# Down projections of two layers by Strassen's seven products, in a hybrid-layer network on one core

## The chip, the cores and the metric

The kernel runs on one core of a Trainium2 chip. The metric is the time of one execution on the device, in microseconds (us); lower is better. Engines are named as the profile names them: PE (TensorE, with PEld for its weight loads), DVE (VectorE), ACT (ScalarE), POOL (GpSimd), SP (SyncE, which issues most transfers here). SBUF is the on-chip memory of all engines, PSUM the one of eight banks that PE writes.

## The reference

512 tokens of width 1024 go through two hybrid layers (chunk attention, a convolution and retention side by side, then an MLP) and then one block of another kind. The change touches the MLP of the two layers:

```python
h = rms_norm(x, g_mlp_pre)                                  # (512, 1024)
f = jnp.square(jax.nn.relu(h @ w_up)) @ w_down              # w_up (1024, 4096), w_down (4096, 1024)
return x + rms_norm(f, g_mlp_post)
```

All is float32. The two layers are computed one after the other, each with its own weights.

## The kernel before

**Products.** PE multiplies float32r operands. To keep float32 accuracy each operand is split in a high part (a rounding copy) and a low part (operand minus high part), and each product is three matmuls: high by high, high by low, low by high. `accumulate` (line 717, matmul in line 723) issues them. A matmul has 128 x 128 stationary numbers and 512 moving columns and adds to one PSUM bank.

**Weights.** They come from memory in units of 128 x 2048 numbers (1 MB), by SP, into two buffers `raw` in turn (`load`, lines 412 to 420). ACT copies a unit to `w_hi` (`hi`, line 1412), then POOL subtracts to give `w_lo` (`lo`, line 534, or in four pieces of 512 columns, `lo_pieces`, line 526) and frees the `raw` buffer with the semaphore `split_ready`, which lets SP load the next unit. There are two `w_hi` and two `w_lo`, so ACT may write one only after PE has read it: `hi("half")` waits until PE is through the first unit of a product, `hi(7)` until bank 7 is full.

**The MLP.** The 4096 hidden features are cut in eight groups of 512. For each group g an "up" makes the hidden features (two units of `w_up`, 8 blocks of 128 inputs, 4 banks: 8 x 4 x 3 = 96 matmuls into banks 0 to 3), and a "down" multiplies them with 512 rows of `w_down` (two units of 512 output columns each; per unit 4 token tiles x 4 blocks x 3 = 48 matmuls into banks 4 to 7). `mlp_order` (line 170) sets PE's order: up(g+1) stands ahead of down(g), so that the other engines have an up's time for the hidden group. The first up (`first_group`, line 815) runs inside the norm before it.

**Beside PE.** DVE rectifies and scales a full bank into `hid` (line 2339), ACT squares it (line 1714) and makes its high part (line 1715), DVE its low part (`low`, line 2169). In the first group of a layer ACT also clears `f` with two copies of 2048 columns (line 1718). After each down DVE adds banks 4 to 7 to `f` in SBUF (line 2353, 128 x 512 each, eight per group). After the last down ACT sums squares (line 1444), DVE makes the scales (lines 2037 to 2041), and PE turns and scales `f` (line 795) into the next norm.

**Order in POOL's queue.** In layer 1 it is one `lo` per unit, in a loop. In layer 2 POOL also computes tables that the later block needs: `output_tables` (line 573) and `turns` (line 604), 37 tensor_tensor operations of 128 x 512 with both inputs in SBUF. They are generators; after each of 18 yields one `lo` follows.

Every engine runs its own list of instructions in order. A wait in it holds all that stands behind it.

```python
def mlp_order(eng, c, up, down, n, per):
    up(0, 0)
    def body(j):
        up(2 * j + 1, 1)
        down(2 * j, 0)
        up(2 * j + 2, 0)
        down(2 * j + 1, 1)
```

Of the kernel before, what the change touches and what calls it, by code (L numbers as in the profile page):

```python
# [13 lines left out]

# [12 lines left out]
P = 128  # L27
# [39 lines left out]
for _name, _w in (("g0", KD), ("g2", KD), ("qg", 1), ("kg", 1), ("subln", 1), ("a_re", NS), ("a_im", NS),  # L67
# [35 lines left out]
PER_PASS = dict(  # L103
    act_step=8, free0=2, free1=2, free2=2, free3=2, free4=4, free5=4, free6=4, free7=4, full0=2,
    full1=2, full2=2, full3=2, full4=4, full5=4, full6=4, full7=4, h_hi=8, h_lo=8, half_done=2,
    split_ready=8, w_loaded0=64, w_loaded1=64)
# [82 lines left out]

def build(nc, a, out):  # L190
# [36 lines left out]
    "f_clear",  # L227
    "table_made",
# [54 lines left out]
def memory(nc):  # L283
# [53 lines left out]
    m.diag = ar("diag", [P, NT, P], 14)  # L337
# [18 lines left out]
    m.h_lo = [ar(f"h_lo{i}", [P, 4, T], 8 + 16 * i, F32R) for i in range(2)]  # L356
    m.both_first = ar("both_first", [P, T], 56)
# [45 lines left out]
def loads(sp, a, m, s, out):  # L403
# [8 lines left out]
    def load(*parts):  # L412

        slot = unit[0] % 2
        unit[0] += 1
        apart(sp, s["split_ready"], c.up("split_ready"), s["slot_seen"])
        for to, of in parts:
            sp.dma_start(to(m.raw[slot]), of).then_inc(s[f"w_loaded{slot}"], 16)
        if beside:
            beside.pop(0)()  # L420
# [13 lines left out]
    def layer(l):  # L434
# [27 lines left out]
        def up(g, _):  # L462
            column_group(a["w_up"], l, g * GROUP)

        def down(g, _):
            for half in range(2):
                load((into(KU, GROUP), rows(a["w_down"], l, g * GROUP, KU, half * GROUP, GROUP)))

        mlp_order(sp, c, up, down, N_UP, PER_PASS)
# [43 lines left out]
def low_parts(pool, m, s):  # L513
# [14 lines left out]

    def lo(n=UNIT):
# [26 lines left out]
    def pre_norm():  # L556

        lo()
        add_squares(1, 2, 3, 4, 5, 6)
        lo()  # L560
# [69 lines left out]
    def layer(l):  # L630
# [12 lines left out]
        pre_norm()  # L643
        if l < DEPTH - 1:
            passes(pool, c, U_MLP // 2 - 2, PER_PAIR, pair)
        else:
            for _ in range(4):
                lo()
            for _ in output_tables():
                lo()  # L650
            lo()
            for _ in turns(0):
                lo()
            for _ in range(U_MLP - 4 - 4 - 15 - 3):
                lo()
        lo()
        lo_pieces()
        pre_norm()

# [34 lines left out]
def products(pe, m, s):  # L694
# [240 lines left out]

    def layer(l):
# [36 lines left out]
        def up(g, i):  # L973
            if isinstance(g, int) and g == 0:
                first_group()
            else:
                feature_major(4)

        def down(g, i):
            pe.wait_ge(s["h_lo"], c.up("h_lo", 4))  # L980
            for half in range(2):
                wh, wl = weights(next_unit(), KU, GROUP)
                for t in range(NT):
                    tt = slice(t * P, (t + 1) * P)
                    accumulate(4 + t, bank[4 + t][:], [(m.h_hi[i][:, k, tt], m.h_lo[i][:, k, tt], wh[:, k, :], wl[:, k, :])
                                                       for k in range(KU)], True, True, False)

        mlp_order(pe, c, up, down, N_UP, PER_PASS)
# [206 lines left out]
NEW, NEW_POST = (5, 6, 7), (4, 5, 6, 7)  # L1195
BUSY = (1, 4, 22, 4)
# [169 lines left out]
def functions(act, a, m, s):  # L1366
# [72 lines left out]
    def post_square(k, x):  # L1439

        if k >= 4:
            act.wait_ge(s["post_squared"], c.at("post_squared") - 3)
        c.up("post_squared")
        act.activation(m.squares[k % 4][:], x, ACT.Square, accum_out=m.half_sums[:, k:k + 1]).then_inc(s["post_squared"], 1)
# [5 lines left out]

    def post_half(squared, copied=None):

        for t in range(NT):
            squared(NT + t)
            if t == 2:
                post_root(0, 2)
            if t == 3:
                post_root(2, 4)
            if copied:
                copied(t)  # L1460
# [34 lines left out]
    def pre_norm(gain):  # L1495

        for k in range(KD):
# [6 lines left out]
            if k == 5:  # L1504
                hi("half")
# [149 lines left out]
    def layer(l):  # L1655
# [45 lines left out]
        post_half(squared, copied)  # L1701
        act.wait_ge(s["layer_loaded"], c.up("layer_loaded", 16))
        pre_norm(gain("g_mlp"))

        def up(g, i):
            use(0, 1, 2, 3)
            if isinstance(g, int) and g == 0:
                act.wait_ge(s["full3"], c.at("full3"))
                hi()
            else:  # L1710
                hi("half")
            for b in range(4):
                freed(b)
                link(act.activation(m.hid[:, b, :], m.hid[:, b, :], ACT.Square))
                act.activation(m.h_hi[i][:, b, :], m.hid[:, b, :], ACT.Copy).then_inc(s["h_hi"], 1)
            if isinstance(g, int) and g == 0:
                for half in range(2):
# [3 lines left out]
        def down(g, i):  # L1721
            hi(7)
            use(4, 5, 6, 7)
            if isinstance(g, int) and g == N_UP - 1:
                for k in range(NT):
                    summed(k)
# [1058 lines left out]
```

## Time and profile before

| | us |
|---|---|
| runs of the kernel: median of 3 (lowest, highest) | 2116.07 (2110.57, 2118.12) |
| the profiled execution, its own time | 2113.84 |
| its span in the trace | 2112.0 |
| PE busy | 2066.0 |
| DVE, ACT, POOL busy | 1033.8, 881.0, 891.0 |
| mean granted TensorE clock, share of full | 0.995 |

The profile is of one execution. "Busy" of PE counts overlapping matmuls once and is not a measure of how full the array is. A row of a group of instructions gives line, engine, operation, output<-input by the program's names, shapes and count, then busy time and mean length, then the idle time of that engine before them and what ended it. A row of the timeline begins with start and length in us; brackets hold the idle time before it.

### The profile page before, as it was taken

Reading aid. Unit: us, or ns where it says so; the run is one execution under the profiler, and the core shown is the slowest. Engines: PE = TensorE matmul, PEld = TensorE weight load, DVE = VectorE, ACT = ScalarE, POOL = GpSimd, SP = SyncE. Lnnn points to the kernel's source line nnn. Section 1 sums busy time; section 2 is a strip of 40 time slices with the busy share of each in tenths; the row PEclk is TensorE's granted clock in tenths of the full one; section 3 lists DMA queues with packets and bytes.
Section 4 is the critical chain, followed back from the end, with each engine's and each line's share of the span. In section 5 each row is a group of like instructions: output and inputs, shape, how many; then the busy total and the mean of one; then the engine's idle time right before and its main releaser. Section 6 shows DMA issues by size and latency. Waiting matters only on the chain.

```text
span 2112.0 us, 27508 instructions
## 1 busy us (share of the span) xinstructions
PE 2066.0 (98%) x10240; PEld 1659.4 (79%) x10240; DVE 1033.8 (49%) x1713; ACT 881.0 (42%) x1257; POOL 891.0 (42%) x282
## 2 busy tenths in 40 slices
PE   8999999999999999999999998999999999999999
PEld 7875888888888775888888886777776787888887
DVE  5866242222236764232222248886589634464555
ACT  5345562223344445542322352265476434333332
POOL 5533244444435323445665446224222344444442
PEclk9999999999999999999999998999999999999999
DMA  5432123322224321223323224232211222332232
GB/s 180 156 110 80 60 81 99 101 90 91 97 75 156 127 90 54 67 100 100 99 89 104 88 83 148 86 90 90 80 61 60 100 100 80 100 99 87 92 99 80
DMA packets 120050, 202.29 MB, mean 96 GB/s; under 512 B 6545, under 2 KB 51857, under 8 KB 119697
## 3 DMA queue, kind: packets, MB, share of 16 engines
q1 hardware_dynamic: 112992, 189.12, 27.3%
q10 hardware_dynamic: 6960, 11.88, 2.0%
q8 instruction: 60, 0.98, 0.2%
q14 instruction: 38, 0.30, 0.0%
HBM read 189.44 MB, written 8.12 MB: 94 GB/s over the span
## 4 chain that ended last, share of the span: by engine, by line
PE 75%; issue 15%; DVE 5%; POOL 3%; ACT 1%; DMA 0%; ACTq 0%; DVEq 0%; POOLq 0%; SPq 0%
PE bank L723 63%; PE bank L837 5%; POOL w_lo L534 3%; PE bank L848 1%; PE bank L795 1%; PE bank L906 1%; PE bank L866 1%; PE bank L894 1%; PE bank L1040 0%; DVE w L2449 0%; DVE pr L2107 0%; PE bank L777 0%; PE bank L932 0%; POOL sums L550 0%; DVE w L2443 0%
## 5 line engine op out<-in xcount | busy, mean ns | idle before, releaser
L534 POOL TENSOR_TENSOR w_lo<-raw,w_hi 128x2048 fp32r<-128x2048 f32 (+1 forms) x167 | 742.2, 4444 | 1151.8 <-ACT w_hi L1412 1151.8
L1412 ACT ACTIVATE w_hi<-raw 128x2048 fp32r<-128x2048 f32 (+1 forms) x170 | 314.3, 1849 | 582.5 <-PE bank L723 528.1
L723 PE MATMUL bank<-act_hi,w_hi 128*128 128x512 f32 x1296 | 516.5, 399 | 3.7 <-DVE hid L2658 2.5
L723 PE MATMUL bank<-act_hi,w_lo 128*128 128x512 f32 x1296 | 506.5, 391 | 0.0
L723 PE MATMUL bank<-act_lo,w_hi 128*128 128x512 f32 x1296 | 506.4, 391 | 0.0
L723 PEld LDWEIGHTS bank<-act_hi,w_hi 128*128 128x128 f32 x1296 | 244.3, 189 | 67.0 <-issue 12.2
L723 PEld LDWEIGHTS bank<-act_hi,w_lo 128*128 128x128 f32 x1296 | 244.2, 188 | 52.4
L723 PEld LDWEIGHTS bank<-act_lo,w_hi 128*128 128x128 f32 x1296 | 244.6, 189 | 49.3 <-issue 1.0
L723 PE MATMUL bank<-w_hi,h_hi 128*128 128x512 f32 x512 | 199.2, 389 | 0.0
L723 PE MATMUL bank<-w_lo,h_hi 128*128 128x512 f32 x512 | 199.2, 389 | 0.0
L723 PE MATMUL bank<-w_hi,h_lo 128*128 128x512 f32 x512 | 199.2, 389 | 0.0
L2353 DVE TENSOR_TENSOR f<-f,bank 128x512 f32<-128x512 f32 x128 | 87.9, 687 | 225.1 <-PE bank L723 225.1
L2339 DVE SCALAR_TENSOR_TENSOR hid<-bank,rrow 128x512 f32<-128x512 f32 x64 | 43.7, 691 | 250.2 <-PE bank L723 245.1
L723 PE MATMUL bank<-w_hi,act_hi 128*128 128x512 f32 (+1 forms) x320 | 120.6, 377 | 0.0
L723 PE MATMUL bank<-w_hi,act_lo 128*128 128x512 f32 (+1 forms) x320 | 117.6, 368 | 0.0
L723 PE MATMUL bank<-w_lo,act_hi 128*128 128x512 f32 (+1 forms) x320 | 117.6, 368 | 0.0
L723 PEld LDWEIGHTS bank<-w_hi,h_lo 128*128 128x128 f32 x512 | 96.1, 188 | 20.0
L723 PEld LDWEIGHTS bank<-w_hi,h_hi 128*128 128x128 f32 x512 | 96.1, 188 | 20.0
L723 PEld LDWEIGHTS bank<-w_lo,h_hi 128*128 128x128 f32 x512 | 96.1, 188 | 19.9
L2653 DVE TENSOR_TENSOR bank<-bank,rrow 128x512 f32<-128x512 f32 x44 | 30.7, 699 | 142.5 <-PE bank L723 139.9
L837 PE MATMUL bank<-act_hi,w_hi 128*128 128x512 f32 x192 | 78.5, 409 | 4.2 <-DVE act_lo L2029 3.4
L2082 DVE SCALAR_TENSOR_TENSOR bank<-ypad,lcol,bank 128x512 f32<-128x512 f32 x116 | 76.6, 753 | 0.0
(393 smaller groups left out, 3078.3 us busy)
## 6 DMA issues: line engine op xcount, KB each, us to landing
raw<-in_w_up SPq DMA_DIRECT2D x32, 1024.0 KB, 5.5
raw<-in_w_down SPq DMA_DIRECT2D x32, 1024.0 KB, 5.0
raw<-in_w_in SPq DMA_DIRECT2D x26, 1024.0 KB, 5.2
raw<-in_w_up SPq DMA_DIRECT2D x44, 512.0 KB, 4.5
raw<-in_w_in SPq DMA_DIRECT2D x28, 768.0 KB, 4.6
raw<-in_w_out SPq DMA_DIRECT2D x12, 1024.0 KB, 5.0
raw<-in_w_down SPq DMA_DIRECT2D x22, 512.0 KB, 4.2
raw<-in_w_attn_proj SPq DMA_DIRECT2D x4, 1024.0 KB, 5.0
```

The source lines that it names most:

```text
L534: pool.tensor_tensor(m.w_lo[slot][:, 0:n], m.raw[slot][:, 0:n], m.w_hi[slot][:, 0:n].bitcast(F32), ALU.subtract).then_inc(s["split_ready"], 1)
L723: mm = pe.matmul(o, ll if i == 2 else lh, rl if i == 1 else rh, start=first and n == 0, stop=last and n == len(steps) - 1)
L795: mm = pe.matmul(bank[b][:, t * P:(t + 1) * P], m.f[:, 4 * (k // 4) + t, k % 4 * P:(k % 4 + 1) * P], m.diag[:, t, :], start=True, stop=True)
L837: mm = pe.matmul(bank[b][:], (wl if i == 2 else wh)[:, k % KU, cols], (m.act_lo if i == 1 else m.act_hi)[:, k, :], start=(k == 0 and i == ...
L848: pe.matmul(bank[b][:] if o is None else o, lhsT, rhs, start=True, stop=True).then_inc(s[f"full{b}"], 1)
L866: mm = pe.matmul(bank[b][head(h), j * P:T], m.rv[:, j, h * HD:(h + 1) * HD], m.pr[:, 2 * (i % 2) + comp, 0:T - j * P], start=(j == 0), sto ...
L894: mm = pe.transpose(bank[6][:, kc * P:(kc + 1) * P], m.pr[:, 2 * (step % 2) + comp, kc * P:(kc + 1) * P], m.ident)
L1412: act.activation(m.w_hi[slot][:, 0:n], m.raw[slot][:, 0:n], ACT.Copy).then_inc(s["w_hi"], 1)
L2082: ins = dve.scalar_tensor_tensor(to, y, w, sums, ALU.mult, ALU.add)
L2339: dve.scalar_tensor_tensor(m.hid[:, b, :], bank[b][:], 0.0, m.rrow[:], ALU.max, ALU.mult).then_inc(s[f"free{b}"], 1)
L2353: dve.tensor_tensor(sums, sums, bank[4 + b][:], ALU.add).then_inc(s[f"free{4 + b}"], 1)
L2653: dve.tensor_tensor(bank[b][:], bank[b][:], m.rrow[:], ALU.mult).then_inc(s["up_scaled"], 1)
```

## The change

In seven of the eight groups of a layer the down projection (512 tokens x 512 features by 512 features x 1024 outputs) is done with Strassen's algorithm in the form with shared sums. Both operands are cut in quarters: h in 256 tokens x 256 features, w_down in 256 rows x 512 columns. Seven products of quarters, or of sums of quarters, take the place of eight. A product is two token tiles x 2 blocks x 3 = 12 matmuls in two banks, 84 for a group. Products 3, 5 and 7 add onto the banks of products 1, 3 and 5 while those still hold their sum, and product 6 onto those of product 4, so the sums of products cost no instruction. DVE adds each bank after each product to `f`: 14 additions for a group. The last group is done as an ordinary product (96 matmuls), now in an order by token tile, with eight banks.

Sums of quarters: four of h (128 x 512 numbers each) and four of w_down (128 x 1024 each), all by DVE, all with both inputs in SBUF. High parts of the seven factors of either operand are made by ACT, low parts of h's factors by DVE, those of w_down's by POOL (128 x 1024 each). The factors of w_down use the halves of the two `w_hi`/`w_lo` buffers as four slots: 0, 1, 2, 3, 0, 1, 2. Slots 2 and 3 are the buffer that the up in front of the down reads to its end.

`mlp_steps` takes the place of `mlp_order`: a loop of six steps and one more, each an up and then a down. Units of `w_down` now hold 256 rows of all 1024 columns. The first unit of an up is split by POOL in four pieces. Layer 2's tables stand in POOL's queue from the second step on, three places for each step: behind factor 0, behind factor 1, and behind the second unit of the next up. ACT's sums of squares in the norms write one scrap tile and wait for each other.

The diff, cut to its core:

```diff
+FACTORS = [((4, 5), 0), ((6, 7), 1), ((4, 5), 2), ((6, 7), 3), ((4, 5), 0), ((6, 7), 1), ((4, 5), 2)]
+SUM_OF = (0, 0, 4, 6, 6, 4, 2)
+def mlp_steps(eng, c, step, last):
+    passes(eng, c, N_UP - 2, PER_STEP, step)
+    last()
 # SP
+        def down(g):
+            for r in range(2):
+                load((into(2, D), rows(a["w_down"], l, g * GROUP + r * 2 * P, 2, 0, D)), loaded="d_loaded")
+        def step(g):
+            column_group(a["w_up"], l, (g + 1) * GROUP)
+            down(g)
 # POOL
+    def factor_lo(n, of):
+        pool.wait_ge(s["w_hi"], c.up("w_hi"))
+        pool.tensor_tensor(half_slot(m.w_lo, n), of, half_slot(m.w_hi, n).bitcast(F32), ALU.subtract).then_inc(s["q_lo"], 1)
+    def mlp_step(beside=(), last=False):
+        factor_lo(0, quarter(m.raw[0], 0))
+        next(beside, None)
+        factor_lo(1, quarter(m.raw[1], 0))
+        next(beside, None)
+        pool.wait_ge(s["t_made"], c.up("t_made", 4))
+        raw_free()
+        factor_lo(2, m.w_sum[0][:])
+        factor_lo(3, m.w_sum[1][:])
+        factor_lo(0, m.w_sum[2][:])
+        factor_lo(1, quarter(m.raw[1], 1))
+        raw_free()
+        factor_lo(2, m.w_sum[3][:])
...
+            lo_quarters(4)
+        lo()
+        next(beside, None)
...
-            for _ in output_tables():
-                lo()
-            lo()
-            for _ in turns(0):
-                lo()
+            tables = itertools.chain(output_tables(), turns(0))
+            for g in range(N_UP - 1):
+                mlp_step(tables if g else (), g == N_UP - 2)
 # PE
+    def down():
+        ready = c.at("h_lo")
+        for p, (banks, n) in enumerate(FACTORS):
+            wh, wl = (half_slot(w, n) for w in (m.w_hi, m.w_lo))
+            if p < 3:
+                pe.wait_ge(s["h_lo"], ready + (p + 1 if p < 2 else 7))
+            pe.wait_ge(s["q_lo"], c.up("q_lo"))
+            for j, b in enumerate(banks):
+                fill(b)
+                tt = slice(j * P, (j + 1) * P)
+                for k in range(2):
+                    for i in range(3):
+                        mm = pe.matmul(bank[b][:], (m.q_lo if i == 2 else m.q_hi)[:, p, k, tt], (wl if i == 1 else wh)[:, k, :],
+                                       start=(p in (0, 1, 3) and k == 0 and i == 0), stop=(k == 1 and i == 2), skip_group_check=True)
+                mm.then_inc(s[f"full{b}"], 1)
 # ACT
+        def step(last=False):
+            act.wait_ge(s["hid_ready"], c.up("hid_ready", 4))
+            h_part(0, x(0, 0))
+            h_part(1, x(1, 0))
+            for p, of in ((3, m.h_sum[:]), (4, x(0, 1)), (2, x(0, 0)), (5, x(1, 0))):
+                act.wait_ge(s["h_sum"], c.up("h_sum"))
+                h_part(p, of)
+            h_part(6, x(1, 1))
+            act.wait_ge(s["half_done"], c.up("half_done"))
+            act.wait_ge(s["d_loaded0"], c.up("d_loaded0", 16))
+            factor_hi(0, quarter(m.raw[0], 0))
+            act.wait_ge(s["d_loaded1"], c.up("d_loaded1", 16))
+            factor_hi(1, quarter(m.raw[1], 0))
+            use(0, 1, 2, 3)
+            for b in range(3):
+                squares(b)
+            act.wait_ge(s["full3"], c.at("full3"))
+            act.wait_ge(s["t_made"], c.up("t_made", 4))
+            factor_hi(2, m.w_sum[0][:])
+            squares(3)
+            factor_hi(3, m.w_sum[1][:])
...
+            done(5, 3)
+            half_hi(0, 0)
+            done(7, 3)
+            half_hi(0, 1)
+            done(5, 4)
+            act.activation(m.w_hi[1][:], m.raw[1][:], ACT.Copy).then_inc(s["w_hi"], 1)
 # DVE
+        def h_factors():
+            link(dve.tensor_tensor(m.h_sum[:], x(0, 1), x(1, 1), ALU.add), "h_sum")
+            link(dve.tensor_tensor(x(0, 1), x(0, 0), x(0, 1), ALU.subtract), "h_sum")
+            h_low(0, x(0, 0))
+            h_low(1, x(1, 0))
+            link(dve.tensor_tensor(x(0, 0), m.h_sum[:], x(0, 0), ALU.subtract), "h_sum")
+            link(dve.tensor_tensor(x(1, 0), x(1, 0), x(0, 0), ALU.subtract), "h_sum")
+            for p, of in ((3, m.h_sum[:]), (4, x(0, 1)), (2, x(0, 0)), (5, x(1, 0)), (6, x(1, 1))):
+                h_low(p, of)
+        def w_factors():
+            wait("d_loaded0", 16)
+            wait("d_loaded1", 16)
+            link(dve.tensor_tensor(m.w_sum[1][:], b12, b11, ALU.subtract), "t_made")
+            link(dve.tensor_tensor(m.w_sum[2][:], b22, b12, ALU.subtract), "t_made")
+            link(dve.tensor_tensor(m.w_sum[0][:], b22, m.w_sum[1][:], ALU.subtract), "t_made")
+            link(dve.tensor_tensor(m.w_sum[3][:], b21, m.w_sum[0][:], ALU.subtract), "t_made")
+        def step(last=False):
+            h_factors()
+            w_factors()
+            for b in range(4):
+                rectify(b)
+            for p in range(7):
+                for j in range(2):
+                    add_factor(p, j)
+                if last and p >= 3:
+                    low(m.l_lo[p - 3][:], m.act2[:, p - 3, :], m.l_hi[p - 3][:], "h_hi", "h_lo")
```

`quarter` and `half_slot` give a quarter of a `raw` buffer and a half of a `w_hi`/`w_lo` buffer, `raw_free` frees a `raw` buffer for SP, `done(b, n)` waits until bank b has been filled n times in this step, `link` waits for the instruction just issued.

## Rows read from the trace of the kernel before

**Rows 1.** The page's busy times (share of the span) and its chain by line

```profile
PE 2066.0 (98%) x10240; PEld 1659.4 (79%) x10240; DVE 1033.8 (49%) x1713; ACT 881.0 (42%) x1257; POOL 891.0 (42%) x282
...
PE bank L723 63%; PE bank L837 5%; POOL w_lo L534 3%; PE bank L848 1%; PE bank L795 1%; PE bank L906 1%; PE bank L866 1%; PE bank L894 1%; PE bank L1040 0%; DVE w L2449 0%; DVE pr L2107 0%; PE bank L777 0%; PE bank L932 0%; POOL sums L550 0%; DVE w L2443 0%
```

**Rows 2.** Timeline of PE and DVE: start, length, instruction

```profile
312.58 0.39 PE L723 MATMUL bank<-w_hi,h_hi 128*128 128x512 f32 x1
...
320.06 0.39 PE L723 MATMUL bank<-w_hi,h_hi 128*128 128x512 f32 x1
...
348.21 0.69 DVE L2339 SCALAR_TENSOR_TENSOR hid<-bank,rrow 128x512 f32<-128x512 f32 x1 [12.91 <-PE bank L723]
...
356.91 2.49 DVE L2169 TENSOR_TENSOR h_lo<-hid,h_hi 128x512 fp32r<-128x512 f32 x4
...
391.66 0.69 DVE L2339 SCALAR_TENSOR_TENSOR hid<-bank,rrow 128x512 f32<-128x512 f32 x1 [12.84 <-PE bank L723]
```

**Rows 3.** Groups by shape, ACT; timelines of ACT and of PE's first up

```profile
L1412 ACT ACTIVATE w_hi<-raw 128x2048 fp32r<-128x2048 f32 x144 | 275.6, 1914 | 534.1 <-PE bank L723 499.8 <-issue 18.5 <-DMA raw<-in_w_in 9.9
...
296.73 0.63 ACT L1715 ACTIVATE h_hi<-hid 128x512 fp32r<-128x512 f32 x1
297.27 3.70 ACT L1718 ACTIVATE f<-kcol 128x2048 f32<-128x2048 f32 x2
...
290.69 0.50 PE L723 MATMUL bank<-act_hi,w_hi 128*128 128x512 f32 x1
```

**Rows 4.** Tile w_lo on POOL: count, ns min/median/max

```profile
L534 POOL TENSOR_TENSOR w_lo<-raw,w_hi x167: 3473/4606/5078, 19.5 to 2088.3; 128x2048 fp32r<-128x2048 f32 x141, 128x1536 fp32r<-128x1536 f32 x26
...
L526 POOL TENSOR_TENSOR w_lo<-raw,w_hi x12: 1281/1290/1609, 10.9 to 1223.8; 128x512 fp32r<-128x512 f32 x12
```

**Rows 5.** Two tiles on DVE: count, ns min/median/max

```profile
L2353 DVE TENSOR_TENSOR f<-f,bank x128: 679/687/690, 315.8 to 1227.6; 128x512 f32<-128x512 f32 x128
...
L2169 DVE TENSOR_TENSOR h_lo<-hid,h_hi x86: 678/684/3967, 293.9 to 2096.2; 128x512 fp32r<-128x512 f32 x86
```

**Rows 6.** Groups by shape, DVE: one line at two widths

```profile
L2107 DVE TENSOR_TENSOR pr<-bank,decay 128x512 f32<-128x512 f32 x12 | 7.7, 686 | 27.3 <-PE bank L848 27.3
...
L2107 DVE TENSOR_TENSOR pr<-bank,decay 128x384 f32<-128x384 f32 x12 | 6.1, 550 | 0.0
```

**Rows 7.** Timeline of DVE and POOL where both have work

```profile
1425.83 5.12 DVE L2494 TENSOR_TENSOR k<-k,rope 128x512 f32<-128x512 f32 x1
...
1425.66 4.73 POOL L534 TENSOR_TENSOR w_lo<-raw,w_hi 128x2048 fp32r<-128x2048 f32 x1 [6.75 <-ACT w_hi L1412]
...
1302.66 1.43 DVE L2492 TENSOR_TENSOR partner<-partner,rope 128x512 f32<-128x512 f32 x1
1304.01 1.54 DVE L2494 TENSOR_TENSOR q<-q,rope 128x512 f32<-128x512 f32 x1
...
1303.50 1.50 POOL L617 TENSOR_TENSOR both<-turn_table,turn_table 128x512 f32<-128x512 f32 x1
```

**Rows 8.** Groups by shape, POOL: busy us, mean ns; a table with a broadcast input

```profile
L595 POOL TENSOR_TENSOR c_part<-ctab,par 128x512 f32<-128x512 f32 x4 | 4.2, 1050 | 0.3
```

**Rows 9.** Timeline of PE, and one us of the windows (third from last: PEclk)

```profile
17.92 0.47 PE L837 MATMUL bank<-act_hi,w_hi 128*128 128x512 f32 x1 [2.38 <-DVE act_lo L2029]
...
19.15 0.63 PE L837 MATMUL bank<-act_hi,w_lo 128*128 128x512 f32 x1
...
22.56 0.39 PE L837 MATMUL bank<-act_lo,w_hi 128*128 128x512 f32 x1
...
620.30 2.05 PE L795 MATMUL bank<-diag,f 128*128 128x128 f32 x16 [0.99 <-DVE diag L2041]
...
21.00:22.00 1.00, 1.00 (x4) 0.81 (x3) 0.55 (x1) 1.00 (x3) 1.00 (x1) 0.50 0.00 0
```

**Rows 10.** The page's transfers: count, size, us to landing

```profile
raw<-in_w_up SPq DMA_DIRECT2D x32, 1024.0 KB, 5.5
raw<-in_w_down SPq DMA_DIRECT2D x32, 1024.0 KB, 5.0
```

More of the change, by code:

```diff
@@ L460, in layer @@
             column_group(a["w_out"], l, g * GROUP)
[L462 to L469, printed above, removed]
+        def down(g):
[4 more added lines that the diff above has]
+            down(g)
+        column_group(a["w_up"], l, 0)
+        mlp_steps(sp, c, step, lambda: step(N_UP - 2))
+        down(N_UP - 1)
     for l in range(DEPTH):
@@ new lines, in last_down, with tile @@
+    def last_down():
+        def tile(i, u, k):
+            t, half = divmod(i, 2)
+            cols, tt = slice(half * SW, (half + 1) * SW), slice(t * P, (t + 1) * P)
+            for n in range(3):
+                mm = pe.matmul(bank[(4 + i) % 8][:], (m.l_lo if n == 2 else m.l_hi)[2 * u + k][:, tt],
+                               (m.w_lo if n == 1 else m.w_hi)[u][:, k * D:(k + 1) * D][:, cols],
+                               start=(u == 0 and k == 0 and n == 0), stop=(u == 1 and k == 1 and n == 2))
+            return mm
+        unit[0] += 1
+        for k in range(2):
+            if k == 0:
+                pe.wait_ge(s["lo_piece"], c.up("lo_piece"))
+            else:
+                pe.wait_ge(s["split_ready"], c.up("split_ready"))
+            pe.wait_ge(s["h_lo"], c.up("h_lo"))
+            for i in (4, 5, 6, 7, 2, 3, 0, 1):
+                if k == 0:
+                    fill((4 + i) % 8)
+                mm = tile(i, 0, k)
+        mm.then_inc(s["half_done"], 1)
+        next_unit()
+        pe.wait_ge(s["h_lo"], c.up("h_lo", 2))
+        for i in range(8):
+            for k in range(2):
+                mm = tile(i, 1, k)
+            mm.then_inc(s[f"full{(4 + i) % 8}"], 1)
@@ L971, in layer @@
         post_norm()
[L973 to L988, printed above, removed]
+        first_group()
+        mlp_steps(pe, c, lambda g: (up(), down()), lambda: (up(), down()))
+        last_down()
         post_norm()
@@ L1740, in functions @@
+        mlp_steps(act, c, lambda g: step(), lambda: step(last=True))
+        c.up("hid_ready", 4)
+        c.up("h_hi", 4)
+        use(0, 1, 2, 3, 4, 5, 6, 7)
+        hi("half")
+        for i in range(8):
+            act.wait_ge(s["f_done"], c.up("f_done"))
+            post_square(i, m.f[:, 4 * (i % 2) + i // 2, :], 4 * (i % 2) + i // 2)
+            if i == 4:
+                post_root(0, 2)
+        post_root(2, 4)
+        pre_norm(gain("g_next"), lambda: hi("half"))
     act.wait_ge(s["eps_loaded"], 16)
@@ L2346, in down @@
-        def down(g, i):
-            for half in range(2):
-                for b in range(4):
-                    freed(4 + b)
-                    full(4 + b)
-                    sums = m.f[:, 4 * half + b, :]
-                    dve.tensor_tensor(sums, sums, bank[4 + b][:], ALU.add).then_inc(s[f"free{4 + b}"], 1)
-                    if isinstance(g, int) and g == N_UP - 1:
-                        freed(4 + b)
-                        dve.sem_inc(s["f_done"], 1)
-                        if half == 1 and b == 2:
-                            post_diag(0, 2)
@@ new lines, in layer @@
+        for b in range(4):
+            rectify(b)
+        wait("f_clear", 2)
+        mlp_steps(dve, c, lambda g: step(), lambda: step(last=True))
+        c.up("hid_ready", 4)
+        c.up("d_loaded0", 16)
+        c.up("d_loaded1", 16)
+        for i in range(8):
+            b = (4 + i) % 8
+            full(b)
+            sums = m.f[:, 4 * (i % 2) + i // 2, :]
+            dve.tensor_tensor(sums, sums, bank[b][:], ALU.add).then_inc(s[f"free{b}"], 1)
+            freed(b)
+            dve.sem_inc(s["f_done"], 1)
+            if i == 4:
+                post_diag(0, 2, 4)
```

232 lines of the change are left out of this document (153 added, 79 removed).

## The prediction

> **What bounds the kernel now.** First the page's busy times and its chain: PE is busy in 98% of the span, the others in 42 to 49%; in the chain that ended last, the matmuls of line 723 alone have 63% [rows 1]. So the time is PE's, and the half-idle engines look like free room: in an average over the span they are. The 0.39 us of a matmul [rows 2] are not its price: matmuls overlap, and in order of time they start every (320.06 - 312.58) / 33 = 0.2267 us [rows 2]. One group (96 up and 96 down matmuls) then takes 192 x 0.2267 = 43.5 us; the same rectify stands at 348.21 and at 391.66 [rows 2], 43.45 apart with a loop end between, so bank changes, waits and loop ends cost PE nothing.
>
> **What the change removes.** Seven products of 12 matmuls take the place of 96, in 7 groups of both layers: 14 x 12 = 168 matmuls, 168 x 0.2267 = 38.1 us. The matmul's shape stays (128 x 128 by 512). A step (up, then down) becomes 180 x 0.2267 = 40.8 us: up 21.8, each product 2.72, down 19.0. The last group stays ordinary.
>
> **What it adds, per step.** ACT takes 1.91 us for 2048 columns and 0.63 for 512 [rows 3], by a line between them 1.06 for 1024. It now has nine pieces of 1024 (seven factors of w_down, two halves of w_up), one of 2048, seven parts of h and four squares: 9.5 + 1.9 + 4.4 + 2.5 = 18.3 us. POOL takes 4.6 and 1.29 (medians [rows 4]), so 2.4 for 1024: seven factors 16.8, four quarters 5.2, one whole unit 4.6, in all 26.6 us, where four units took 18.5. DVE: 14 adds and 4 rectifies at 0.69 [rows 2, 5], 7 low parts of h at 0.61 (four took 2.49 [rows 2]), 4 sums of h at 0.72 (0.69 and a hand-over, since each is waited for), and 4 sums of w of 1024 columns, not in the trace: 0.686 for 512 and 0.550 for 384 [rows 6] give 0.136 per 128 columns, 1.23 in all; bounds 0.69 (no longer than 512) and 1.37 (twice it). That is 18 x 0.69 + 11 x 0.66 + 4 x 1.23 = 24.6 us. By these totals every engine has room under PE's 40.8.
>
> **What stands against hiding.** A DVE instruction with both inputs in SBUF doesn't run beside a POOL tensor_tensor. One of 0.69 took 5.12: it began 0.17 after a POOL piece of 4.73 and ended 0.56 after it [rows 7]. Where both have work queued they alternate: DVE's 0.69 takes 1.43 and 1.54, POOL's 1.05 takes 1.50, and in turn one ends 0.91 and the other 0.55 after the one before [rows 7]. A low part of h has once taken 3.97; the 128 adds that read PSUM lie between 0.679 and 0.690, so they are never held [rows 5]. Today four low parts per group lie clear of POOL. The change puts 15 such instructions (4 sums and 7 low parts of h, 4 sums of w) into each up, where three of POOL's pieces must come too. By the Trainium skill, page SBUF — State Buffer, section Who interferes with whom, a DVE instruction with two SBUF inputs and a GpSimd one that reads SBUF exclude each other for the whole instruction, and with one SBUF input don't contend; by that rule sharing is impossible in all these pairs, and the trace agrees.
>
> **Chain of a plain step**, laid out from those durations in each engine's own order, in us from the start of up. PE's last bank of the down before is seen after 0.46, when ACT makes w_hi of slot 1, to 2.4; POOL, held 0.2 by a sum of h, 2.6 to 7.2. DVE's seven low parts and two linked sums wait for it: 7 x 0.61 + 2 x 0.72 = 5.7, to 12.9. POOL's factor 0 (ACT has it at 12.4) 12.9 to 15.1; first sum of w to 16.3; factor 1 to 18.5; three sums of w, 3.7, to 22.2. Only now can DVE rectify the new h, which its order puts behind the sums: three banks take 1.9, to 24.0 (PE had filled them at 13.6 to 19). ACT squares the third, to 24.7, and turns to factor 2, which its order puts behind those squares: to 25.7. POOL makes the low part, to 28.2. PE wants it after up and two products, 21.8 + 5.4 = 27.2. Stall 1.0, and 0.2 for loading the weights: **1.2**. If the sums of w all came ahead of factor 1, they would end 2.3 earlier and nothing would be late: the low bound is 0. With POOL a tenth slower (2.6 for 1024) it is 3.3, the high one. Later factors have slack: each is wanted 2.72 after the one before, POOL makes one in 2.4.
>
> The first step of a layer starts behind the clearing of f: two of 1.9 from 297.27, with four h_hi copies of 0.63 before them gone [rows 3], end 8 us after the start of up (290.69 [rows 3]). Behind them come the 11 instructions of DVE on h (7.2), factors 0 and 1 (2.3 each), the sums of w (4.9), three rectifies (1.9), a square (0.6), ACT's and POOL's part of factor 2 (1.1 + 2.5): 30.8, with hand-overs 31.2, which is 4.0 late; **4.2**.
>
> **Layer 2's tables.** POOL also computes 37 table operations there of 1.05 (a broadcast input [rows 8]) or 1.29 us (as a piece of 512 [rows 4]), before beside whole units, now six in each of steps 2 to 7: two behind the unit of 4.6, two behind factor 0, two behind factor 1. Five of them come in turn ahead of the last sum of w. Five times 1.05 is 5.2; I take 4.5, since ACT is ready a little later too. That stall is 1.0 + 4.5 + 0.2 = **5.7**. Step 2 has no pair behind the unit and waits 1.8; the last 5.5. Bounds: 1.0 per step if the two engines never leave the shared access idle (POOL 26.6 + 7.0, DVE 12.5, less 33 overheads of 0.69 - 0.56 = 0.13 [rows 7], is 41.8 against 40.8), and 6.5 if all six count.
>
> Stalls: layer 1 4.2 + 6 x 1.2 = 11.4; layer 2 4.2 + 1.8 + 4 x 5.7 + 5.5 = 34.3; 45.7 in all.
>
> **The clock.** After 2.38 us of idle PE the starts went from 0.23 to 0.43 apart from 19.15 to 22.56, the granted clock at 0.50, that is 1.2 GHz, and 2.4 GHz again from there by the lengths of 0.39 [rows 9]. Eight matmuls lose 0.2 each, 1.6 in all. A wait of 0.99 stands in the trace with 16 matmuls of 128 columns in 2.05 behind it, 0.13 each, too fast for half the clock [rows 9]; so I let plain stalls lose nothing. Seven stalls are over 3 us: 7 x 1.6 = 11.2; bounds 0 and 8 x 1.6.
>
> **At nothing.** Weights: a load lands 5.0 to 5.5 us after issue [rows 10]; w_down's second unit, asked for at 7.4, is there at 12.7, when ACT comes to it; the tightest is the next group's second, free behind factor 5 at 35.4, there 41.2, wanted at 42.5. If late, 1 us per step. The loads' rows are longer, their bytes the same. Squares one after another in the norms: banks fill every 2.7 us, a square with its read takes 0.8. The last down keeps 96 matmuls; its tail is add, square, root, diag as before (the 0.99 [rows 9]). Bounds -1 and +3 in all.
>
> **Sum.** -38.1 + 45.7 + 11.2 = +18.8. The profiled execution took 2113.84, span 2112.0; so 2132.6. The runs' median is 2.2 higher, inside their spread of 7.5; I say 2133.
>
> **Rivals.**
> Everything hides (the totals decide): if alternation lets DVE's sums through early, no stall stays, 2113.8 - 38.1 = 2076, up to 2090 with the two first steps. For it: the totals. Against: DVE held for whole pieces [rows 7]. Chance 0.15.
> Half: plain steps hide, since 1.0 is small beside 27, and the tables find gaps at 2.5 per step with no clock loss: -38.1 + 8.4 + 15 = -15, 2099. Chance 0.12.
> Level: stalls as worked out, but no clock loss or shorter table stalls: 2113.8 + 3 = 2117 (2104 to 2124). Chance 0.18.
> Forecast, 2124 to 2146: chance 0.42.
> Worse: port overheads add up, every plain step loses 3.3 as with slower POOL (+14 per layer), and next loads come late: 2133 + 28 = 2161, from 2146 on. Chance 0.13.
> That the change does not save its matmuls I give nothing: 84 against 96 is written in the table of products.
>
> About 0.5%, 10.6 us, is what a measurement of this kernel tells from no change. Faster: 0.15 + 0.12 = 0.27; same 0.18; slower 0.55. The range leaves out the first rival and the worst part of the last: 2094 to 2152. The forecast's own is 2124 to 2146.
>
> **What would show it.** PE has 10072 matmuls, busy share some 95%. Right: PE idle ahead of the third product's first matmul, put down to POOL's w_lo; about 1 us in layer 1, 5 to 6 in layer 2, and 4 in each first step; matmuls 0.43 apart behind the long ones; DVE's sums of w with means near 2 us instead of 1.23; layer 2's steps near 48 us, layer 1's near 42. Wrong: steps of 40.8 in both layers (port not binding); DVE's two-SBUF instructions at 0.69 beside POOL; stalls at another product or ahead of up (loads or the next unit late); no 0.50 clock in layer 2.

## The result and the profile after

The changed kernel took **2128.8 us** (median of 5 runs, 2125.79 to 2135.43), the kernel before 2115.45 beside it (5 runs): a ratio of **1.0074**, 95% interval 1.0049 to 1.0098. The change is slower, by 0.7%, though it takes 168 matmuls out. The profiled execution took 2128.65, its span is 2126.9, 14.9 more than before's 2112.0.

The page of the changed kernel, busy times and chain by engine, against [rows 1]:

```profile
PE 2043.2 (96%) x10072; PEld 1634.9 (77%) x10072; DVE 1348.1 (63%) x1951; ACT 942.4 (44%) x1385; POOL 1041.4 (49%) x396
...
PE 58%; issue 21%; DVE 14%; POOL 5%; ACT 2%; ACTq 0%; DVEq 0%; DMA 0%; POOLq 0%; SPq 0%
```

and the chain by engine of the kernel before:

```profile
PE 75%; issue 15%; DVE 5%; POOL 3%; ACT 1%; DMA 0%; ACTq 0%; DVEq 0%; POOLq 0%; SPq 0%
```

The matmuls are gone, and yet the span has grown: DVE and POOL, 8% of the chain before, now have 19%. The waits of PE say where (engine, line, waited for: us in all, times, longest), of the whole span and then of each layer's MLP:

```profile
PE bank L1042 <- POOL w_lo L574: 33.2, 12, 5.1
PE bank L1042 <- issue: 4.9, 3, 2.6
...
PE bank L1042 <- POOL w_lo L574: 6.9, 6, 3.3
PE bank L1042 <- issue: 0.6, 1, 0.6
...
PE bank L1042 <- POOL w_lo L574: 26.3, 6, 5.1
PE bank L1042 <- issue: 4.3, 2, 2.6
```

So 7.5 us of idle PE in layer 1 and 30.6 in layer 2, all ahead of the third product's first matmul but one stall: in layer 2's last step PE waits 2.59 ahead of the second product and then 1.74 ahead of the third. One place of each layer, in the timeline of PE:

```profile
404.26 0.50 PE L1042 MATMUL bank<-w_hi,q_hi 128*128 128x512 f32 x1 [0.72 <-POOL w_lo L574]
404.60 0.39 PE L1042 MATMUL bank<-w_lo,q_hi 128*128 128x512 f32 x1
...
1063.35 0.79 PE L1042 MATMUL bank<-w_hi,q_hi 128*128 128x512 f32 x1 [5.14 <-POOL w_lo L574]
1063.94 0.63 PE L1042 MATMUL bank<-w_lo,q_hi 128*128 128x512 f32 x1
1064.37 0.63 PE L1042 MATMUL bank<-w_hi,q_lo 128*128 128x512 f32 x1
```

Behind the stall of 0.72 the next matmul starts 0.34 after the first and the one after that 0.23 later, as at full speed. Behind 5.14 they start 0.43 apart (the first even 0.59), and the granted clock of the window (third number from the end) is the lower level, 1.2 GHz:

```profile
1064.00:1066.00 2.00, 2.00 (x6) 0.50 0.00 0
```

53 matmuls of the two MLPs are slow in this way, 7 behind layer 1's first stall and 46 in layer 2: 53 x 0.2 = 10.6 us.

The span by stretches, from the same landmarks in both traces (times in us from the span's start, the kernel before's in brackets): the first up of layer 1 starts 2.5 earlier than before (288.19 against 290.69 [rows 3]); the norm's second token matmuls close layer 1's MLP at 609.90 (620.30 [rows 9]), 7.9 gained in that MLP; the same place of layer 2 is at 1244.92 (1230.37), 25.0 lost since; 0.4 more to the end. -2.5 - 7.9 + 25.0 + 0.4 = 15.0, the 14.9 of the spans with rounding. **Layer 1 gains what layer 2 more than loses**, although both layers run one code on PE, ACT and DVE; only POOL's differs, by the tables. A step takes 41.8 us in layer 1 and 48.0 in layer 2, for 180 x 0.2267 = 40.8 of matmuls.

How the stall of a layer 2 step comes about, in the timelines of DVE, POOL and ACT:

```profile
1095.50 2.07 DVE L2544 TENSOR_TENSOR w_sum<-raw 128x1024 f32<-128x1024 f32 x1
1097.61 2.20 DVE L2545 TENSOR_TENSOR w_sum<-raw,raw 128x1024 f32<-128x1024 f32 x1
1099.84 3.30 DVE L2546 TENSOR_TENSOR w_sum<-raw,w_sum 128x1024 f32<-128x1024 f32 x1
1103.18 1.96 DVE L2547 TENSOR_TENSOR w_sum<-raw,w_sum 128x1024 f32<-128x1024 f32 x1
1105.26 2.48 DVE L2522 SCALAR_TENSOR_TENSOR act<-bank,rrow 128x512 f32<-128x512 f32 x4
...
1094.99 1.50 POOL L675 TENSOR_TENSOR c_part<-ctab,par 128x512 f32<-128x512 f32 x1
1096.57 2.15 POOL L676 TENSOR_TENSOR ctab<-ctab,c_part 128x512 f32<-128x512 f32 x1
1098.80 3.26 POOL L574 TENSOR_TENSOR w_lo<-raw,w_hi 128x1024 fp32r<-128x1024 f32 x1
1102.02 2.03 POOL L669 TENSOR_TENSOR ctab<-ctab,par 128x512 f32<-128x512 f32 x1
1104.13 1.91 POOL L670 TENSOR_TENSOR c_part<-ctab,par 128x512 f32<-128x512 f32 x1
1108.83 2.36 POOL L574 TENSOR_TENSOR w_lo<-w_sum,w_hi 128x1024 fp32r<-128x1024 f32 x1 [2.78 <-ACT w_hi L1846]
...
1105.98 1.82 ACT L1843 ACTIVATE act<-act 128x512 f32<-128x512 f32 x3 [12.74 <-DVE act L2522]
1107.71 1.04 ACT L1846 ACTIVATE w_hi<-w_sum 128x1024 fp32r<-128x1024 f32 x1
```

The two engines take turns through all of it: by starts and lengths each instruction ends 0.9 to 1.2 us behind the other engine's (2.3 for POOL's low part of 1024 columns), and DVE's four sums of w take 9.5 us. Behind the last sum there follow, in series, the rectifies, three squares of ACT, its copy to 1108.8 and POOL's low part to 1111.2; PE starts at 1111.32. In layer 1 there is nothing on POOL beside the last two sums, and by groups of its six steps (count | busy us, mean ns) they show their true length:

```profile
L2544 DVE TENSOR_TENSOR w_sum<-raw 128x1024 f32<-128x1024 f32 x6 | 20.5, 3420 | 0.0
L2545 DVE TENSOR_TENSOR w_sum<-raw,raw 128x1024 f32<-128x1024 f32 x6 | 19.8, 3301 | 0.2
L2546 DVE TENSOR_TENSOR w_sum<-raw,w_sum 128x1024 f32<-128x1024 f32 x6 | 7.3, 1225 | 0.2
L2547 DVE TENSOR_TENSOR w_sum<-raw,w_sum 128x1024 f32<-128x1024 f32 x6 | 7.3, 1225 | 0.2
```

Layer 2's last step is another case. Between POOL's factor 0 and factor 1 four table operations stand there, not two: `output_tables` ends without a yield, so the same place also takes the first two operations of `turns`. Factor 1 (1198.39) is done at 1201.62, and the second product's first matmul starts at 1201.71:

```profile
1190.58 1.50 POOL L675 TENSOR_TENSOR c_part<-ctab,par 128x512 f32<-128x512 f32 x1
1192.15 2.15 POOL L676 TENSOR_TENSOR ctab_end<-ctab_end,c_part 128x512 f32<-128x512 f32 x1
1194.49 1.83 POOL L691 TENSOR_TENSOR sin_n<-turn_table,turn_table 128x512 f32<-128x512 f32 x1 [0.18 <-POOL ctab_end L676]
1196.27 2.04 POOL L692 TENSOR_TENSOR both_first<-turn_table,turn_table 128x512 f32<-128x512 f32 x1
1198.39 3.23 POOL L574 TENSOR_TENSOR w_lo<-raw,w_hi 128x1024 fp32r<-128x1024 f32 x1
...
1201.71 0.47 PE L1042 MATMUL bank<-w_hi,q_hi 128*128 128x512 f32 x1 [2.59 <-issue]
```

### The profile page after: what moved, and what is told of

Same layout as the page of the kernel before. It is cut to its first block, busy times and chain, and to the rows that moved or that the text cites. A ratio compares the mean times of both kernels' runs of the same rounds, so it can differ in the third digit from the quotient of the medians.

```text
span 2126.9 us, 28005 instructions
## 1 busy us (share of the span) xinstructions
PE 2043.2 (96%) x10072; PEld 1634.9 (77%) x10072; DVE 1348.1 (63%) x1951; ACT 942.4 (44%) x1385; POOL 1041.4 (49%) x396
## 4 chain that ended last, share of the span: by engine, by line
PE 58%; issue 21%; DVE 14%; POOL 5%; ACT 2%; ACTq 0%; DVEq 0%; DMA 0%; POOLq 0%; SPq 0%
PE bank L795 33%; PE bank L1042 10%; PE bank L909 5%; POOL w_lo L610 3%; DVE q_lo L2354 3%; PE bank L1053 2%; DVE w_sum L2544 2%; DVE w_sum L2545 1%; PE bank L920 1%; POOL w_lo L574 1%; DVE w_sum L2546 1%; PE bank L1022 1%; DVE w_sum L2547 1%; PE bank L867 1%; PE bank L978 1%
## 5 line engine op out<-in xcount | busy, mean ns | idle before, releaser
L610 POOL TENSOR_TENSOR w_lo<-raw,w_hi 128x2048 fp32r<-128x2048 f32 (+1 forms) x123 | 541.4, 4402 | 853.9 <-ACT w_hi L1542 840.6
L795 PE MATMUL bank<-act_hi,w_hi 128*128 128x512 f32 x1072 | 428.8, 400 | 3.6 <-DVE hid L2883 2.5
L795 PE MATMUL bank<-act_lo,w_hi 128*128 128x512 f32 x1072 | 418.9, 391 | 0.0
L1542 ACT ACTIVATE w_hi<-raw 128x2048 fp32r<-128x2048 f32 (+1 forms) x112 | 203.2, 1815 | 268.0 <-PE bank L795 194.2
L795 PEld LDWEIGHTS bank<-act_lo,w_hi 128*128 128x128 f32 x1072 | 202.3, 189 | 40.9 <-issue 1.0
L1042 PE MATMUL bank<-w_hi,q_hi 128*128 128x512 f32 x392 | 159.4, 407 | 38.1 <-POOL w_lo L574 33.2
L574 POOL TENSOR_TENSOR w_lo<-w_sum,w_hi 128x1024 fp32r<-128x1024 f32 x56 | 133.1, 2397 | 78.3 <-ACT w_hi L1846 75.4
L1042 PE MATMUL bank<-w_lo,q_hi 128*128 128x512 f32 x392 | 157.5, 402 | 0.0
L1042 PE MATMUL bank<-w_hi,q_lo 128*128 128x512 f32 x392 | 157.1, 401 | 0.0
L574 POOL TENSOR_TENSOR w_lo<-raw,w_hi 128x1024 fp32r<-128x1024 f32 x42 | 115.4, 2755 | 72.2 <-ACT w_hi L1846 71.7
L2354 DVE TENSOR_TENSOR q_lo<-act,q_hi 128x512 fp32r<-128x512 f32 x84 | 122.8, 1515 | 3.1 <-ACT q_hi L1849 2.9
```

Of the source, the lines that this page charges most:

```text
L574: pool.tensor_tensor(half_slot(m.w_lo, n), of, half_slot(m.w_hi, n).bitcast(F32), ALU.subtract).then_inc(s["q_lo"], 1)
L610: pool.tensor_tensor(m.w_lo[slot][:, 0:n], m.raw[slot][:, 0:n], m.w_hi[slot][:, 0:n].bitcast(F32), ALU.subtract).then_inc(s["split_ready"], 1)
L795: mm = pe.matmul(o, ll if i == 2 else lh, rl if i == 1 else rh, start=first and n == 0, stop=last and n == len(steps) - 1)
L1042: mm = pe.matmul(bank[b][:], (m.q_lo if i == 2 else m.q_hi)[:, p, k, tt], (wl if i == 1 else wh)[:, k, :], start=(p in (0, 1, 3) and k == ...
L1542: act.activation(m.w_hi[slot][:, 0:n], m.raw[slot][:, 0:n], ACT.Copy).then_inc(s["w_hi"], 1)
L2354: dve.tensor_tensor(to, of, hi_part.bitcast(F32), ALU.subtract).then_inc(s[name], 1)
```

## The experiments

All start from the changed kernel, except the control, which starts from the kernel before. The kernel before ran beside each group: its medians were 2116.74 (first four), 2115.77 (next two) and 2113.73 (last two). Theory (A in the expectations): the third product waits for a chain in series, whose sums of w are stretched by turns with POOL because both operands lie in SBUF, and the tables add turns. Rivals (B, another in each experiment): POOL simply has too much work; the tables only fill idle time; the slow matmuls wait for something else.

**The factor ahead of the squares** (e1)

```diff
-            for b in range(3):
-                squares(b)
             act.wait_ge(s["full3"], c.at("full3"))
             act.wait_ge(s["t_made"], c.up("t_made", 4))
             factor_hi(2, m.w_sum[0][:])
-            squares(3)
+            for b in range(4):
+                squares(b)
             factor_hi(3, m.w_sum[1][:])
```

> ScalarE copies the third product's factor (the first sum of w) before it squares the rectified tiles, and no longer after three squares; nothing else is changed. Theory A (the third product waits for a chain in series: VectorE's sums of w, the rectifies, three squares, the copy, GpSimd's subtraction): 3 to 4 us leave the chain in each step, so layer 1's stalls of 0.7 us go and layer 2's of 5.1 us fall to 1.5 to 4 us; about 18 us less than the changed kernel's 2128.8, near 2111, a little under the kernel before. Theory B (GpSimd has too much work in a step whatever the order): layer 2's stalls stay within 1 us of 5.1, the time falls by under 6 us.

Measured: **2101.25** (6 runs), ratio to before 0.9926 (0.9908 to 0.9943). Four lines moved on one engine turn the change from a loss into a gain. PE's waits for w_lo over the whole span:

```profile
PE bank L1042 <- POOL w_lo L574: 13.7, 7, 2.7
```

Layer 1 keeps one stall (0.85, the first step's), layer 2's plain ones fall from 5.1 to at most 2.7; the last step's 2.59 and 1.74 stay. DVE's sums are as long as they were (the step at 1076.31: 2.07, 2.19, 3.30, 1.96), POOL has the same work. So the order did it, and POOL's load as such doesn't bound. The size was off: 27.6 us less, not 18. Idle time in the two MLPs fell by 20, from 38.1 to 18.0 (layer 1's first stall too, from 3.28 to 0.85, which I had not counted), and 41 of the 53 slow matmuls went, another 8.

**No tables** (e2)

```diff
-            tables = itertools.chain(output_tables(), turns(0))
+            tables = zeros()
```

Left out: the second block's table values; `zeros` fills their tiles with zeros, three memsets at the third place of a step.

> The 37 operations by which GpSimd makes the second block's tables beside layer 2's steps are left out; 12 fills with zeros stand in their place, after each step's last subtraction. Theory A (the tables and VectorE's sums lengthen each other by taking turns, and a table operation stands ahead of the factor's subtraction): layer 2's steps become layer 1's, 41.8 to 42.5 us in place of 48.0, its MLP near 323 us in place of 354.2, and the time near 2098 (30 us less). Theory B (layer 2 waits for its own sums and copies, the tables only fill idle time): under 8 us less, 2121 or more.

Measured: **2100.37** (4 runs), ratio 0.9926 (0.9909 to 0.9943), 28.4 less than the changed kernel. Layer 2's stalls become 3.67, then 0.80 or 0.81 in each step, and a step 41.9. So the tables are the whole difference of layer 2's plain steps from layer 1's (41.8), as expected, and the last step's stall went with them (0.59 is left).

**One operand out of SBUF** (e3). Left out: the sums of w have other values.

```diff
-            link(dve.tensor_tensor(m.w_sum[1][:], b12, b11, ALU.subtract), "t_made")
+            p = m.quad[:, 0:2, :]
+            link(dve.tensor_tensor(m.w_sum[1][:], b12, p, ALU.is_gt), "t_made")
...
+            if p == 0:
+                pe.wait_ge(s["t_made"], c.up("t_made", 4))
             if p < 3:
```

`quad` names PSUM banks. The other three sums change likewise; none reads another sum any more.

> The four sums of quarters of w keep their size and their output but read the second operand from two PSUM banks, and compare in place of subtracting; the first product waits for them so that the banks hold still. The values of w's sums are not the reference's. Theory A (two operands in SBUF let VectorE and GpSimd run only in turn): the sums fall from a mean of 2.2 to 2.6 us (layer 1: 3.4, 3.3, 1.2, 1.2) to about 1.2 us each in both layers; layer 1's stalls go, layer 2's fall from 5.1 to 1 to 3 us, and the time to about 2090. Theory B (the length is that of 128x1024 elements and its queue, not the second operand's place): the sums keep 2.2 us or more beside GpSimd and the time stays within 6 us of 2128.8.

Measured: **2081.58** (4 runs), ratio 0.9843 (0.9822 to 0.9866). The four sums in layer 2's steps, by groups, with the tables and POOL's low parts beside them as before:

```profile
L2547 DVE TENSOR_TENSOR w_sum<-raw,bank 128x1024 f32<-128x1024 f32 x6 | 7.3, 1208 | 0.0
L2548 DVE TENSOR_TENSOR w_sum<-raw,bank 128x1024 f32<-128x1024 f32 x6 | 7.3, 1221 | 0.2
L2549 DVE TENSOR_TENSOR w_sum<-raw,bank 128x1024 f32<-128x1024 f32 x6 | 7.3, 1221 | 0.2
L2550 DVE TENSOR_TENSOR w_sum<-raw,bank 128x1024 f32<-128x1024 f32 x6 | 7.3, 1220 | 0.2
```

From 9.5 us to 4.9 in each step, same size, same queue, same neighbours: what stretched them was the second operand's place. (The comparison is no quicker in itself: with nothing beside it a subtraction took 1.225, see layer 1's groups.) With that alone, the squares and tables where they were, no product waits over 0.2 us for w_lo any more, and the time is 8 less than expected; what PE now waits for the sums themselves is 1.8 in all, in the two first steps. The rule of the Trainium skill that the prediction drew on (SBUF — State Buffer, Who interferes with whom) has two halves: two SBUF inputs beside POOL contend, one doesn't. The runs agree with both: 1.96 to 3.42 us beside POOL with two, 1.21 to 1.22 with one.

**Dummies ahead of the stall** (e4)

```diff
+            if p == 2 and dummies:
+                busy(16)
             pe.wait_ge(s["q_lo"], c.up("q_lo"))
```

with `dummies` set in layer 2 alone. `busy(16)` issues 16 matmuls of 128 columns on the identity (two records each in the trace, x32).

> In layer 2 only, TensorE runs 16 matmuls of 128 columns on the identity (0.275 us each) ahead of its wait for the third product's factor. Theory A (the 8 to 10 slow matmuls after each of layer 2's stalls are the half clock that follows an idle TensorE): the first matmuls after the stall keep 0.227 us, 7 x 0.2 = 1.4 us back in each of the steps that stall by 5 us, less up to 2.2 us in the one step whose stall is shorter than the dummies; 4 to 8 us less, near 2123. Theory B (the slow matmuls wait for something else, as the weights' arrival): they stay at 0.43 us, and the time is the same or 2 to 3 us longer.

Measured: **2125.26** (5 runs), ratio 1.0036 (1.0021 to 1.0050). Timeline of PE:

```profile
1103.33 3.84 PE L885 MATMUL bank<-cmat 128*128 128x128 f32 x32 [0.43 <-DVE act L2524]
1108.06 0.49 PE L1044 MATMUL bank<-w_hi,q_hi 128*128 128x512 f32 x1 [0.90 <-POOL w_lo L574]
1108.39 0.39 PE L1044 MATMUL bank<-w_lo,q_hi 128*128 128x512 f32 x1
1108.62 0.40 PE L1044 MATMUL bank<-w_hi,q_lo 128*128 128x512 f32 x1
```

The stall is as long as it was (0.43 + 3.84 + 0.90 = 5.17), but the matmuls behind it are 0.23 apart; steps take 46.3 instead of 48.0. From layer 1's norm landmark to layer 2's it takes 628.3 against 635.0. So the slow matmuls were the clock behind an idle PE. The medians show only 3.5 us of these 6.7, just under the 4 to 8 that I expected, and the intervals of the two ratios overlap, so here the trace decides and not the time: the profiled run of this kernel came to layer 1's first stall 3.5 later than the changed kernel's.

**First and moved** (e5): e1's order, and 4 pairs of tables ahead of layer 2's first step, 7 behind its MLP, one behind each later step.

```diff
         factor_lo(0, quarter(m.raw[0], 0))
-        next(beside, None)
         factor_lo(1, quarter(m.raw[1], 0))
-        next(beside, None)
...
+            some(tables, 4)
...
         lo_pieces()
+        if l == DEPTH - 1:
+            some(tables, 7)
         pre_norm()
         lo()
```

> The factor is copied first, and the table operations leave the places where they stood ahead of a factor's subtraction: 4 pairs go into GpSimd's 8.1 us of idle time ahead of layer 2's first step, one pair stays behind the last subtraction of each of five steps, 7 pairs go into the 14.4 us of idle time while layer 2's norm begins, and 2 behind the norm. The output is the reference's. Theory A (what is left of layer 2's stalls, 14.9 us of idle time and 12 slow matmuls, comes from the tables' taking turns with VectorE's sums): layer 2 stalls as layer 1 does, 1 to 3 us in all, and the time is 2084 to 2088. Theory B (the tables were in idle time, and moving them only moves a wait): the norm behind layer 2 or the second block's first products start 5 us or more later, and the time stays at 2095 to 2101.

Measured: **2096.7** (5 runs), ratio 0.9909 (0.9895 to 0.9922): a miss for theory A's number, and inside theory B's range, though not by B's way: the norm behind layer 2 waits 2.20 instead of 1.07, not 5 more. The later stalls of layer 2 were 0.3, but the first was 5.43 with 11 slow matmuls; and of the 20.0 us between this span and that of e6 (the experiment below), 6.7 had arisen before layer 1's first stall, in the kernel's start (last section). The four pairs ran on POOL from 894.24 to 904.17, 9.9 us where 8.1 had been idle, and DVE was not idle there. The first two sums of h in that step, first here, then in the run without tables (e6):

```profile
895.69 1.28 DVE L2536 TENSOR_TENSOR h_sum<-act 128x512 f32<-128x512 f32 x1 [6.46 <-ACT f L1918]
897.00 1.67 DVE L2537 TENSOR_TENSOR act<-act 128x512 f32<-128x512 f32 x1
```

```profile
889.05 0.69 DVE L2543 TENSOR_TENSOR h_sum<-act 128x512 f32<-128x512 f32 x1 [6.46 <-ACT f L1925]
889.78 0.69 DVE L2544 TENSOR_TENSOR act<-act 128x512 f32<-128x512 f32 x1
```

**First and none** (e6): e1's order and e2's zeros, as a bound for what moving the tables can give.

> The factor is copied first and the 37 table operations are left out (12 fills with zeros in their place), as a bound for the run beside it. Theory A: both layers stall by 1 to 2 us in all and the time is 2080 to 2084, the time of the run in which no two operands of w's sums lay in SBUF (2081.6). If it is over 2090, the turns that the two engines take cost more than the stalls that the records show.

Measured: **2076.91** (5 runs), ratio 0.9829 (0.9814 to 0.9843). That is 3 less than the 2080 to 2084 expected. In the MLPs PE stalls 0.85 and 1.27 in the first steps, no other, and no slow matmul is left. The 38.1 of the removed matmuls are there: 2115.77 - 2076.91 = 38.9, and 33 to 39 by the ratio's interval.

**Moved again** (e7): e5's first group goes ahead of the norm before layer 2's MLP, where DVE's long instructions read PSUM. Seven pairs stand there, five behind the MLP and one behind the last subtraction of each of five steps.

```diff
         for _ in range(4):
             lo()
+        if l == DEPTH - 1:
+            tables = itertools.chain(output_tables(), turns(0))
+            some(tables, 7)
         pre_norm()
```

> As the run with the factor first and the tables moved, but the first group of table operations no longer stands beside VectorE's sums of h in layer 2's first step (where the record showed the sums stretched from 0.7 to 1.7 us each and a stall of 5.4 us): 7 pairs go into GpSimd's 14.4 us of idle time ahead of layer 2's first norm, 5 into the like time behind its MLP, one behind the last subtraction of each of five steps. The output is the reference's. Theory A (a table operation costs only where VectorE works on two operands in SBUF): the first step's stall falls to 1.3 us without slow matmuls, and the time is 2080 to 2088. Theory B (what the tables cost has to be paid somewhere): the time stays at 2094 to 2098.

Measured: **2087.88** (5 runs), ratio to before **0.9869** (0.9850 to 0.9887): nothing is left out here, and it is 1.3% under the kernel before. PE's waits for w_lo:

```profile
PE bank L1050 <- POOL w_lo L574: 2.8, 4, 1.3
```

Layer 2's first stall is 1.30, with no slow matmul. In the spans 8.2 us stay to e6 (2083.3 and 2075.1; this profiled run is the fastest of its five, the medians are 11.0 apart). 1.5 of them had arisen before layer 1's first stall. 1.0 lie between layer 1's norm and layer 2's first stall: the tables are not free in their new place either, for DVE's `diag` in that norm has both inputs in SBUF, and PE waits 1.6 for it instead of 0.3. The row here and in e6:

```profile
846.82 1.21 DVE L2235 TENSOR_TENSOR diag<-cmat,small 128x256 f32<-128x256 f32 x1
...
845.66 0.42 DVE L2241 TENSOR_TENSOR diag<-cmat,small 128x256 f32<-128x256 f32 x1
```

4.4 lie between layer 2's first stall and its norm: 0.9 at that norm's diag, some 2 as starts 0.1 to 0.5 late at the third and fourth products of steps that still hold a pair, the rest not placed. The last 1.3 lie behind that norm.

**Control** (e8): the kernel before, with the same zeros for tables.

> The kernel before with the same 37 table operations left out and the 12 fills with zeros in their place, as a control. Theory A (before the change the tables stood in idle time of GpSimd and beside a VectorE with little work on two SBUF operands): within 4 us of the kernel before's 2116. If it is 15 us or more faster, then the 24 us between the changed kernels with and without tables were not of the change's making.

Measured: 2115.37 (10 runs), ratio 1.0002 (0.9988 to 1.0016). Before the change the same tables cost nothing that shows, 3 us at most by the interval.

## Why the prediction was right

2133 was forecast, 2128.8 measured, in the case that it called likeliest and, but for one step of 14, by the way that it laid out. Part of how close the number came is luck: the clock's term and the start's, below.

- **Removed**: -38.1. PE has 10072 matmuls, and e6 gives the size.
- **Plain steps**: 1.2 each forecast. Measured 41.8 - 40.8 = 1.0, of it 0.72 as idle time. The way was the one laid out: in the step of layer 1 whose up starts at 376.18, the sums end at 21.9 (22.2 laid out), ACT's copy at 25.5 (25.7), POOL's low part at 28.0 (28.2). The prediction's low bound (all sums ahead of factor 1) didn't come. Its high bound, 3.3, doesn't add up: a tenth on the unit and three factors that stand in the chain is 1.2 us, which gives 2.4.
- **First steps**: 4.2 each; 3.28 and 3.71 measured as idle time, 3.6 and 4.0 with 0.3 for the restart. In layer 1 the clearing of f ended 7.6 after the start of up, not 8.
- **Layer 2**: 5.7 a step and 1.8 in step 2; measured 5.14 and 2.23. With the clock, 5.7 + 1.6 = 7.3 against 48.0 - 40.8 = 7.2. The last step, 5.5 forecast, shows 2.59 and 1.74. Here the way was not the one laid out: the prediction put two table operations between factors 0 and 1 where the code has four, so factor 1 was late for the second product. A stall at another product stood among its signs of being wrong, and this is one.
- **Clock**: 7 x 1.6 = 11.2 forecast, 53 x 0.2 = 10.6 measured, from seven stalls as said, but with step 2's 2.23 (8 slow matmuls) in the place of the last step's 2.59 (none). e4 shows that it was the clock. That each stall over 3 us would lose its 1.6 came from one wait, and it is no rule (last section): so this term is right in part by luck. Nor did rows 9 show that 0.13 for a matmul of 128 columns is too fast for half the clock, as a quarter of the slow 0.43 is 0.11. It was so all the same: in e5 the same matmuls behind the wait of 2.20 came to start 0.21 apart, with a granted clock of 0.50, and 0.11 apart before.
- **At nothing**: right for the loads (w_up lands in 5.6, w_down in 5.0, and PE waits for none in the MLPs) and for the norms' tails (0.4 in all). The start, up to layer 1's first up, gave 2.5 by chance: its wait for act_lo was 1.04 against 2.38 [rows 9], and matmuls that were slow behind it before were not. All this lies in the first 23 us, and no code of the change is there.

The sum: -38.1, idle time 38.1, slow matmuls 10.6, 4.5 for 15 restarts, and the start -2.5 make +12.6, of 14.9. A restart costs some 0.3 beside its idle time: 0.16, since idle time counts from a matmul's end, 0.39 after its start, where the next start is due after 0.23; and 0.11 for the next start at 0.34. Of the 2.3 left, 1.2 are five of layer 2's restarts at the lower clock (0.54 to 0.59 instead of 0.34); 1.1 are not placed. The forecast had +18.8. Its stalls were 3.1 too dear in all (45.7 against 38.1 + 4.5), spread over first, plain and last steps, and the start's 2.5 came by chance.

The rivals: "everything hides" (2076 to 2090) is what e3, e6 and e7 reach; the totals of busy time were right, and only the order and the shared access stood between. "Half" fell on the plain steps, which did not hide (1.0 each), and both it and "level" on layer 2's stalls, 5.14 each with the lower clock behind them. "Worse" wanted 3.3 in each plain step and loads that come late; neither came.

One thing the prediction did not see: how cheap the loss was to undo. It had the squares in the chain, but took the order as given.

## What to carry to other kernels

Before moving work onto an engine that the page shows half idle, list where both operands of its instructions lie. Where DVE reads two SBUF operands beside POOL, add the two engines' times instead of taking the larger, and put table work where DVE mostly reads PSUM, not merely where POOL is idle. Then follow the one chain that the bound engine (here PE) waits for and put its links at the head of each queue: here the order alone (e1) was worth 27.6 us, and with the tables moved (e7) 40.9.

## What had not been expected of the hardware

- POOL is stretched by the turns too. A table operation of 1.05 us [rows 8] took 1.91 in layer 2's steps of the changed kernel, by groups:

```profile
L670 POOL TENSOR_TENSOR c_part<-ctab,par 128x512 f32<-128x512 f32 x4 | 7.7, 1914 | 0.3
```

- The clock's fall is no function of a stall's length alone. In the changed kernel a stall of 2.23 was followed by 8 slow matmuls and one of 2.59 by none; in e1 2.45 by 7, and of three stalls of 2.69 the first by 5 and the others by none. One and the same stall, the 3.28 of layer 1's first step, was followed by 7 in the changed kernel and by none in e2, while in e7 a wait of 1.97, in the norm behind layer 2, was followed by the lower level. Windows of e2 (the stall ends at 322.26) and of e7 (the wait ends at 1200.22), granted clock third from the end:

```profile
324.00:326.00 2.00, 2.00 (x10) 1.66 (x9) 1.30 (x2) 0.65 (x1) 2.00 (x2) 1.00 0.03 8
...
1202.00:1204.00 2.00, 2.00 (x11) 2.00 (x11) 1.90 (x4) 1.72 (x4) 1.82 (x3) 0.50 0.00 0
```

  What decides was not tried.
- The start of the kernel differs from execution to execution by several us, whatever the code behind it: the wait for act_lo in the first norm was 1.04, 2.38, 3.88 and 5.52 us in the profiled runs of the changed kernel, the kernel before, e2 and e5, with the lower clock behind the three longer ones; in e7 and e8 it was 2.40 and 2.42 with no slow matmul behind it. With one and the same order of work behind it, layer 1's first stall came at 315.97 (e6) and at 322.63 (e5), 6.7 us apart, as much as the runs of one kernel spread.
